# Causal mask by VectorE, three PSUM banks exchanged, and unscaled input rows with the norm's root applied to the products, in a two-layer decoder step

## The reference, cut to what matters

```python
z = rmsnorm(x, g1) @ w_in                     # rmsnorm: x * rsqrt(mean(x*x) + EPS) * g1
u, va = gelu(z[:, :512]), rmsnorm(gelu(z[:, 512:1024]), av_g)
q, k, v = rmsnorm(z_q), rmsnorm(z_k), z_v     # q and k normed per head half of 64
s_a = chunk_mix(va)                           # per 128 rows, a lower-triangular 128 x 128 matrix per head
p = softmax(where(kpos <= qpos, q @ k.T * 0.125, -1e30))   # two score maps per head (m = 0, 1)
o_b = (p0 - lam * p1) @ v
x = x + concat(u * s_a, rmsnorm(o_b)) @ w_out
x = x + hierarchical_moe(rmsnorm(x, g2))      # 16 experts, top 2, rows gathered and scattered through HBM
```

## Time and profile before

| what | value |
|---|---|
| median of 3 runs | 1022.73 us (1018.94 to 1022.89) |
| profiled execution | 1022.66 us |
| its span, first to last instruction | 1020.8 us |
| PE busy | 962.5 us (94%) |
| PE weight loads | 495.4 us (49%) |
| DVE busy | 440.4 us (43%) |
| ACT busy | 233.3 us (23%) |
| POOL busy | 191.5 us (19%) |

### The profile page before, as it was taken

The page is one execution under the profiler, slowest core; times in us unless marked ns, Lnnn a source line. Parts: engine busy times, 40 slices in busy tenths (PEclk is TensorE's granted clock), DMA queues, the critical chain, the costliest instruction groups (busy, mean ns, idle before and its releaser), DMA issues.

```text
span 1020.8 us, 13578 instructions
## 1 busy us (share of the span) xinstructions
PE 962.5 (94%) x4918; PEld 495.4 (49%) x4918; DVE 440.4 (43%) x1154; ACT 233.3 (23%) x483; POOL 191.5 (19%) x265
## 2 busy tenths in 40 slices
PE   6999999999998999999599999999989989999991
PEld 4444455556456444434254344655555554444340
DVE  2403122566346466551343111345563565555523
ACT  2101255542001011111121114555220011111110
POOL 2333201331101111111125031022220011111100
PEclk9999999999998999999899999999999999999996
DMA  8716003342511979998742150134252059799946
GB/s 335 267 31 257 1 1 129 103 146 91 220 42 63 383 259 370 420 421 328 240 144 83 49 209 1 68 109 160 63 208 103 21 222 367 274 381 412 403 153 209
DMA packets 39769, 197.72 MB, mean 194 GB/s; under 512 B 7632, under 2 KB 7760, under 8 KB 23824
## 3 DMA queue, kind: packets, MB, share of 16 engines
q1 hardware_dynamic: 19744, 136.22, 34.0%
q0 software_dynamic: 15888, 45.87, 12.8%
q10 hardware_dynamic: 4064, 14.68, 4.0%
HBM read 177.35 MB, written 29.88 MB: 203 GB/s over the span
## 4 chain that ended last, share of the span: by engine, by line
PE 84%; DVE 6%; DMA 4%; issue 2%; POOL 1%; ACT 1%; POOLq 0%; SPq 0%; ACTq 0%; DVEq 0%
PE ps L673 77%; PE ps L671 6%; DMA cat<-y_rows 1%; DMA x<-in_xp 1%; POOL st L517 1%; PE ps L688 1%; DMA y_rows<-hn,isca 1%; DVE cat L1720 1%; DVE hT L1393 0%; DMA hT<-h_rows,igat 0%; DVE tmp L1542 0%; DVE st L1543 0%; ACT hn L1306 0%; DVE st L1510 0%; DVE o_sb L1530 0%
## 5 line engine op out<-in xcount | busy, mean ns | idle before, releaser
L673 PE MATMUL ps<-ring,hT 128*128 128x512 f32 (+2 forms) x1056 | 382.4, 595 | 2.9 <-DVE hT L1393 2.5
L673 PEld LDWEIGHTS ps<-ring,hT 128*128 128x128 f32 (+2 forms) x1056 | 148.9, 166 | 198.1 <-issue 196.9
L673 PE MATMUL ps<-ring,cat 128*128 128x512 f32 (+2 forms) x560 | 195.4, 596 | 2.6 <-ACT hn L1306 2.4
L673 PEld LDWEIGHTS ps<-ring,cat 128*128 128x128 f32 (+2 forms) x560 | 72.9, 162 | 82.3 <-issue 79.4
L617 POOL DMA_INDIRECT y_rows<-hn,isca x28 | 28.1, 1003 | 250.1 <-ACT hn L1306 219.5
L673 PE MATMUL ps<-hT,ring 128*128 128x512 f32 (+1 forms) x256 | 71.8, 437 | 0.3 <-ACT cat L1194 0.3
L515 POOL TENSOR_SCALAR st<-st 128x1 f32<-128x1 f32 (+3 forms) x60 | 16.3, 272 | 282.2 <-ACT sqj L1150 106.4
L517 POOL TENSOR_TENSOR st<-st,half 128x1 f32<-128x1 f32 (+3 forms) x60 | 62.5, 1042 | 11.6 <-POOL st L515 11.1
L1861 DVE TENSOR_TENSOR hT<-ps,par 128x512 f32<-128x512 f32 x56 | 36.0, 685 | 56.0 <-PE ps L671 55.6
L1414 DVE TENSOR_REDUCE st<-sqj 128x8 f32<-128x512 f32 x20 | 13.5, 681 | 108.3 <-ACT sqj L1165 108.2
L1306 ACT COPY hn<-ps 128x1024 f32<-128x1024 f32 x28 | 28.4, 1013 | 118.3 <-PE ps L673 118.3
(11 more groups left out here) (249 smaller groups left out, 1172.7 us busy)
## 6 DMA issues: line engine op xcount, KB each, us to landing
ring<-in_w SPq DMA_DIRECT2D x82, 1024.0 KB
kc<-in_w SPq DMA_DIRECT2D x12, 1024.0 KB
vc<-in_w SPq DMA_DIRECT2D x10, 1024.0 KB
v<-in_w SPq DMA_DIRECT2D x10, 1024.0 KB
kva<-in_w SPq DMA_DIRECT2D x10, 1024.0 KB
kc<-in_ck POOLq DMA_DIRECT2D x32, 256.0 KB, 3.6
vc<-in_cv POOLq DMA_DIRECT2D x32, 256.0 KB, 3.2
h_rows<-qk ACTq DMA_DIRECT2D x10, 512.0 KB, 2.6
```

The costliest lines, as they stand in the source:

```text
L673: ins = pe.matmul(out, lhsT, rhs, start=start, stop=stop, skip_group_check=loose)
```

## The change

- **Input rows.** PE turns `x` itself, with no `scaled` before it. The root multiplies the products instead: by ACT on the way out of the bank for k, v, q and va (a scale per row), and for the transposed gates u by DVE, which multiplies bank F by a row of roots into `tmp`; ACT's gelu then reads `tmp`. The row of roots on all partitions (`roots`) is made after the keys: DVE scales the identity by each tile's roots (`diagonals`), PE multiplies ones by them into T0 and T1, DVE copies them.
- **Layer change.** PE's identity products wait for the last scatter, and are nine; DVE adds a tile and turns the one before it.
- **Causal mask.** The four mask products are gone; DVE adds the mask in PSUM before the maximum.
- **Banks.** `OT[0]` and `OT[1]`, `OT[2]` are exchanged (T1, T1, T0 for T0, T0, T0), and mix(3) uses T1 for F. ACT's turned probabilities come first in the steps that have a `pT`.
- Tile 1 is loaded ahead of the second weight piece; the output tile 3 is turned one product later; ACT takes the gelus of u0 and u1 after its key and query copies.

```diff
-        OT = {t: spare_turn(4 * t + 9) if t < TP - 1 else f"T{t % 2}" for t in range(NT)}
+        OT = {0: "T1", 1: "T1", 2: "T0", TP - 1: "T1", TP: "T0"}
+        MIX_IN = {t: "F" for t in range(NT)}
+        MIX_IN[TP - 1] = spare_turn([n for n, works in SMALL.items() if ("mix", TP - 1) in works][0])
...
+                    if i == 1 and l == 0:
+                        x_load(1)
...
             def turn_half(stage, t, hf):
-                rows = x[:, t, :] if stage == "x" else hn[:, t % 2, :]
+                rows = x[:, t, :]
...
                 if l:
-                    pe.wait_ge(x_ready.sem, l * NT + 1)
-                    keep_busy(10)
+                    Count.layer = l - 1
+                    pe.wait_ge(*y_out[(NSLOT - 1) % 2].at("y", "m", NSLOT - 1))
+                    Count.layer = l
+                    keep_busy(9)
+
+                def turn_input(t):
+                    if l == 0:
+                        pe.wait_ge(*dve_s.at("blank"))
+                        pe.wait_ge(x_in[t].sem, 16)
+                    turn_rows("h1", t, (x_ready.sem, l * NT + (t + 1)))
...
                 rows("k", 0)
+                pe.wait_ge(*dve_s.at("diagonals"))
+                for t in range(NT):
+                    u, n = ("T0", P) if t < TP else ("T1", NROW)
+                    if t in (0, TP):
+                        claim(u)
+                    mm(bank(u)[:, t % TP * P:t % TP * P + n], ones, diagonals[:, t * P:t * P + n], inc=full[u].inc("roots") if t >= TP - 1 else None)
                 rows("v", 1)
...
-                        mm(bank(u, m)[:, 0:(i + 1) * P], qT[m * DK:(m + 1) * DK, h, here], kT[m * DK:(m + 1) * DK, h, 0:(i + 1) * P])
-                    for stay, move in ((B_ID, B_CAUSAL), (B_SWAP, B_SWAP_CAUSAL)):
-                        for m in range(2):
-                            r = slice(m * DK, (m + 1) * DK)
-                            mm(bank(u, m)[:, here], c16[r, stay], c16[r, move], start=False, loose=True,
-                               inc=full[u].inc("s", n) if (m == 1 and stay == B_SWAP) else None)
+                        mm(bank(u, m)[:, 0:(i + 1) * P], qT[m * DK:(m + 1) * DK, h, here], kT[m * DK:(m + 1) * DK, h, 0:(i + 1) * P],
+                           inc=full[u].inc("s", n) if m else None)
...
-                    if (n, k) == (1, 1):
+                    if (n, k) == (1, 2):
                         turn_out(TP - 1)
...
-                        nc.scalar.copy(dst[:, t, :], bank(u)).then_inc(*read[u].inc("z", name, t))
+                        nc.scalar.mul(dst[:, t, :], bank(u), stat["rs"][:, t:t + 1]).then_inc(*read[u].inc("z", name, t))
...
+                    if n in PT_STEPS:
+                        probs_turned(n - 2)
...
+                vec.memset(ones, 1.0)
+                for t in range(NT):
+                    dve.wait_ge(*pool_c.at("rs1", t))
+                    ins = vec.tensor_scalar(diagonals[:, t * P:(t + 1) * P], ident, stat["rs"][:, t:t + 1], None, ALU.mult)
+                ins.then_inc(*dve_s.inc("diagonals"))
...
+                def scale_gates(name, j):
+                    dve.wait_ge(*full["F"].at(name, j))
+                    if name == "us":
+                        out, src = (a.rearrange("p (m t) -> p m t", m=4)[:, :, 0:NROW] for a in (tmp[:, 0:4 * NROW], bank("F")))
+                        by = across(roots[:, TP * P:TP * P + NROW], 4, NROW)
+                    else:
+                        out, src, by = tmp[:, :], bank("F"), roots[:, 0:TP * P]
...
+                    vec.tensor_tensor(out, src, by, ALU.mult).then_inc(*read["F"].inc(name, j))
...
                     b0 = FIRST[f"S{n % 2}"]
+                    diagonal = ps[:, b0:b0 + 2, i * P:(i + 1) * P]
+                    link(vec.tensor_tensor(diagonal, diagonal, across(c16[:, B_CAUSAL], 2, P), ALU.add))
                     link(vec.tensor_reduce(stat["mx"][:, c:c + 2], ps[:, b0:b0 + 2, 0:(i + 1) * P], AX.X, ALU.max))
...
-                for t in range(NT + 4):
-                    if 2 <= t < NT + 2:
-                        add_high(t - 2)
+                for t in range(NT + 1):
+                    if t < NT:
+                        add_high(t)
```

More of the change, by code:

```diff
@@ L262, in program @@
                   v[:, 0:TP, :].rearrange("p t n -> p (t n)"), kva[:, 0:TP, :].rearrange("p t n -> p (t n)")]
+        diagonals = hn[:, 0, 0:NT * P]
+        roots, ones = hn[:, 1, 0:TOK], hn[:, 1, TOK:TOK + P]
         rows_of = sb("rows_of", [P, NT, E, 4], BF16)
@@ L1185, in _ @@
                 square_heads("q", TP, "S0", LOW)
[L1186 to L1187 removed]
+                nc.scalar.mul(qz[LOW, TP, :], bank("S0")[LOW, :], stat["rs"][LOW, TP:TP + 1])
+                nc.scalar.activation(kva[HIGH, TP, :], bank("S0")[HIGH, :], ACT.Gelu_apprx_tanh, scale=stat["rs"][HIGH, TP:TP + 1]).then_inc(*read["S0"].inc("z", "qva"))
                 act.wait_ge(*read["S0"].at("z", "qva"))
@@ L1266, in _ @@
                         probs(n)
-                    if 2 <= n < len(ATT) + 2:
+                    if 2 <= n < len(ATT) + 2 and n not in PT_STEPS:
                         probs_turned(n - 2)
@@ L1434, in _ @@
                 vec.tensor_reduce(stat["lam"][:, 0:2], groups(tmp[:, 0:2 * DK], 2, DK), AX.X, ALU.add).then_inc(*dve_s.inc("lamdot"))
-                link(vec.memset(hn[:, :, :], 0.0))
+                dve.wait_ge(*full["T0"].at("roots"))
+                vec.tensor_copy(roots[:, 0:TP * P], bank("T0")).then_inc(*read["T0"].inc("roots"))
+                dve.wait_ge(*full["T1"].at("roots"))
+                vec.tensor_copy(roots[:, TP * P:TP * P + NROW], bank("T1")[:, 0:NROW]).then_inc(*read["T1"].inc("roots"))
+                link(vec.memset(hn[:, 0, :], 0.0))
                 for t in range(2, NT):
@@ L1487, in mix @@
                 def mix(t):
-                    dve.wait_ge(*full["F"].at("mix", t))
+                    u = MIX_IN[t]
+                    dve.wait_ge(*full[u].at("mix", t))
                     bs = par[:, PAR["bs"]].rearrange("p (c t) -> p c t", c=4)
                     n = NROW if t == TP else P
-                    s, o = (a.rearrange("p (c t) -> p c t", c=4)[:, :, P - n:P] for a in (bank("F"), tmp[:, :]))
+                    s, o = (a.rearrange("p (c t) -> p c t", c=4)[:, :, P - n:P] for a in (bank(u), tmp[:, :]))
                     bs = bs[:, :, 0:n]
@@ L1500, in mix @@
                         dve.wait_ge(*dve_s.at("mix", t - 1))
-                    vec.tensor_tensor(added, part, bs, ALU.add).then_inc(*read["F"].inc("mix", t))
-                    dve.wait_ge(*read["F"].at("mix", t))
+                    vec.tensor_tensor(added, part, bs, ALU.add).then_inc(*read[u].inc("mix", t))
+                    dve.wait_ge(*read[u].at("mix", t))
                     vec.tensor_tensor(catT[:, 0:4, t * P:t * P + n], o, catT[:, 0:4, t * P:t * P + n], ALU.mult).then_inc(*dve_s.inc("mix", t))
@@ L1612, in _ @@
                             add_out(*j)
+                        elif name != "va":
+                            scale_gates(name, j)
+                    if n == 3:
+                        dve.wait_ge(*act_s.at("us", 0))
+                        link(vec.memset(hn[:, 1, :], 0.0))
                     for name, j in SMALL.get(n, []):
@@ L1682, in _ @@
                 turned(0)
+                scaled(0)
                 head_turned(TP - 1)
-                scaled(0)
                 add_out(1, 1)
```

68 lines of the change are left out of this document (35 added, 33 removed).

## The result

| what | before | after |
|---|---|---|
| median | 1021.43 us (6 runs, 1018.94 to 1022.89) | 1028.37 us (6 runs, 1026.21 to 1029.68) |
| ratio to before | | 1.0071, 95% [1.0055, 1.0087] |
| profiled execution, its span | 1022.66, 1020.8 us | 1029.64, 1027.9 us |
| PE busy | 962.5 us | 966.3 us |
| DVE, ACT busy | 440.4, 233.3 us | 455.7, 240.2 us |

What follows compares the result with a forecast made beforehand. The prediction took PE's stream, 84% of the chain that ended last, as the bound. Terms -1.0 +4.0 -4.0 +2.8 +0.4 gave +2.2; with clock losses of 1.5 and 1.0, +4.7: 1027.4, said as 1027 us, range 1013 to 1036.

Steps and rivals of the forecast that it cites:

- forecast case: Whole kernel: slower, with one or two clock losses, own range 1023 to 1031 us; chance 0.45.
- +2.2: Whole kernel: sum in us of the start, roots, layer change and attention terms, before any clock loss.
- Start, -1.0: Kernel start: the second tile's transposes no longer wait for DVE's scaling, 1.0 us gained.
- Roots' products, layer 0, +4.0: After layer 0's keys: PE waits 2.9 us for the diagonals, then 1.1 us of products; cost 4.0 us.
- Layer 1 has the same slip: After layer 1's keys: PE waits 1.7 us for the diagonals, products take 1.1; cost 2.8 us.
- Change of layer, -4.0: Between layers: warm-up waits only for the last scatter, first product at 511.65 instead of 515.68; 4.0 us gained.
- The attention, +0.2 a layer: Attention steps: mask products saved, DVE additions, bank waits and output turn together cost 0.2 us a layer.
- T1 wait: Last attention step: the last head's transposes wait until DVE has read mix(3) from T1; cost 1.7 us a layer.
- later output turn: Attention's end: turning the output one product later fills a PE wait, 0.8 us gained a layer.
- The clock, +2.5: Half clock after layer 0's roots' wait, 1.5 us, and an even chance of 2 at the layer change, taken as 1.0.
- "clearly slower" rival: Last attention step: two waits of 1.9 us also lower the clock in both layers, 1031 to 1037 us; chance 0.15.
- Faster rival: Claims of F and T1: 0.46 us of slack each keeps the mask addition off PE's path, 1011 to 1014; chance 0.15.

Runs made afterwards that it cites:

- e2: The kernel before with one edit: DVE adds the causal mask in place of PE's four mask products per step; 1024.48 us, ratio 1.0039.
- e10: e5 with nine unread identity products ahead of mix(3), in PE's wait there; 1015.43 us, ratio 0.9946.
- e9: The kernel after with seven unread identity products ahead of mix(3) and seven ahead of the last turn_probs, in both layers; 1023.56 us, ratio 1.0030.
- e3: The kernel after with the layer-change warm-up products written into T0 without a claim of bank J; 1027.83 us, ratio 1.0077.
- e5: The kernel after with the edits of e1, e3 and e4 together, and eleven warm-up products instead of nine; 1018.54 us, ratio 0.9985.
- e8: e5 with the mask given back to PE's products in all 16 steps, DVE adding none; 1014.01 us, ratio 0.9942.
- e11: e6 with seven unread identity products ahead of mix(3), in PE's wait there; 1014.14 us, ratio 0.9934.
- e7: e5 with DVE's mask addition made twice in every step; 1022.81 us, ratio 1.0024.
- e6: e5 with the mask given back to PE's products in steps 3, 7, 11 and 15; 1013.74 us, ratio 0.9935.
- e4: The kernel after with the diagonals' wait and the five roots' products moved behind the next four value products, both layers; 1022.43 us, ratio 1.0028.
- e1: The kernel after with mix(3) put back in bank F instead of T1; 1022.6 us, ratio 1.0028.

## Why the prediction was right, and where its steps were off

1027 was forecast and 1028.4 measured, inside the forecast case's own 1023 to 1031. The direction and the main places (the roots' waits, the claims of F, the two waits of the tail) were right. That the number came so near is in part luck. The terms for the layer change and the attention promised 1.9 and 0.3 too much gain. Against that, the roots cost 1.1 less than forecast, the start gave 0.2 more, and 0.8 was saved behind PE's last product, a place that the forecast didn't have. Without the clock this makes +2.3 for +2.2. The clock added 4.7 for 2.5, mostly at other places. Measured against the profiled 1022.66, 1029.64 is 7.0 more, for 4.7 forecast.

- **Start, -1.0.** The second tile's wait is gone, but it belonged to the profiled execution: e2 has the old start, ACT had the second tile's row at 13.99 instead of 15.36, DVE scaled it at 16.47 instead of 17.84, and there was no wait. A gain was booked from one execution's DMA arrival. From start to start it was 1.2: from the first product to the last tile's first one it took 29.3 us for 30.5. Against it stands the first product, 1.03 later. It was at 12.29 and 12.71 in the two kernels with the old start, and between 12.36 and 13.81 in those with the new one. In both kinds it comes late where the clock was granted in full late: 8.80 us and 12.29 in before, 9.03 and 12.36 in e10, 10.07 and 12.71 in e2, 11.24 and 13.32 in after, 12.00 and 13.81 in e9. So this 1.03 goes with the clock of the execution, and no trace shows a start that the edit itself made later.
- **Roots' products, layer 0, +4.0.** Right in kind. The diagonals were ready at 46.72 (46.6 to 46.8 forecast), but two f32 products are four records, 1.72 us, and I had counted 0.86, so the keys ended at 44.4 and the wait was 2.25 instead of 2.9. From 44.4 to 47.95 it is 3.6. Layer 1 has the same slip: from 548.6 to 550.75 it is 2.1, of which 1.2 are the products, for 2.8. The five scalings took 0.93 for my 0.9. The Trainium skill's 58 cycles and half the columns ("VectorE: DVE Perf Modes", the section on the TRN2 errata) would give, as an estimate, 0.65 for the five, so the trace stands against it.
- **Change of layer, -4.0.** The step that failed. I read ACT's load issues at 503.50 in the earlier trace rows as the moment the warm-up could start, and priced "the scatter has landed" without asking what else `keep_busy` waits for. The claim of J made it -2.1; the missing 1.9 is what e3's first product gains (11.55 us from scatter to product, 13.41 in after). With the claim gone and warm-up products that reach up to the transposes, e5 gets -4.5.
- **The attention, +0.2 a layer.** From the roots' products up to mix(2) the changed kernel gained 0.3 a layer, where I had 0.7 (the list without the T1 wait and without the later output turn, which stand behind mix(2)). The mask products were worth 0.11 to 0.12 a step instead of 0.21, and I had booked seven of them as gain: 0.6 to 0.7 too much. The places were right: waits at F in steps 4, 8 and 12, and the old wait in step 9 to 10 gone. The later output turn was worth 0.86 a layer, for 0.8. The T1 wait was right to 0.2: the tail is longer by 1.5 at full clock (e9), for +1.7. ACT's copies with a root take 0.68 instead of 0.58, the squares 0.69 instead of 0.60; I had called them the same form. The Trainium skill has it ("ScalarE: Activation LUTs", What ACT_TABLE_LOAD costs): each per-partition operand adds about 93 ns. The rows agree, with 0.09 to 0.10 us. No wait of PE in the projections came with it, so nothing hung on it.
- **The clock, +2.5.** Both the size and the places were off. Neither the roots' wait (2.25 us in the midst of dense products) nor the layer change in after cost clock. The tails did, 1.6 and 3.1 (19.79 and 21.36 against e9's 18.2), which was the mechanism of the "clearly slower" rival. That rival had 1031 to 1037, because I added its price on top of a clock loss that didn't come. The late full clock at the start cost 1.0. And 1.4 came back in layer 0's experts stage: half clock at 317 in the earlier trace rows lasted from 316.0 to 322.8, in after from 321.9 to 325.3. e8, e9 and e11 have none there and take 246.8 to 246.9 us for the stage, after 247.5; before took 249.7, of which 0.86 is the output turn. Layer 1's experts lost 0.4 in the same way. Part of what a profile shows as gain or loss is thus which execution it is.
- **Faster rival.** It needed slack of 0.46 per claim. There was none: without the addition (e8) the waits for F are 2.4 us a layer shorter, and a second one (e7) lengthens them by 3.6 of the 3.7 us that it takes at the eight claims.

The verdict on the change by its parts: input rows, layer change and later output turn, well placed and with the mask left to PE (e8), are worth 6 us by the medians; how much of that is the clock of other stages isn't separated. DVE's mask addition in all steps costs 0.5 us per layer in waits at the tail and next to nothing in the body, and two or three times that through the clock; with the wait filled (e10) it is as fast as PE's mask within the error. e6, the mix of both, beats the kernel before by 0.65%.

## What to carry to other kernels

Before booking the gain of an earlier start, list every wait in front of the moved instruction, the bank claims too, and who releases them behind what else. On a PE-bound kernel a wait of about two microseconds can have a second price behind it, the clock; filling it with products that nobody reads is a cheap experiment and can be a cheap remedy (-4 us in e9 and in e10, nothing in e11, where the wait was 1.7). The worth of removed small products is read from start to start between their neighbours with and without them, not from their own starts.

## What was not expected of the hardware

- The same two waits of 1.7 us, 2 us apart, left the clock in full in one layer and brought it to half in the other of one execution (e4). In the traces of the kernels whose tail has a single wait of 1.7 (before, e6, e8) it fell in one of six tails; with one unfilled wait of 2.3 to 2.8, or two of 1.7, in 12 of 14; with the waits filled (e9, e10, e11) in none of six. That activity and not place decides is also what the Trainium skill says ("TensorE: Matmul & The Clock Gate", What's actually happening), and these counts agree; e4 shows that they don't settle the single case. They come from one execution of each kernel.
- The roots' wait, 2.1 to 2.3 us in the midst of dense 128x512 products, left the clock in full in all four traces that have it (after, e1, e3, e9). So the length of a wait alone doesn't decide.
- In e3's profile the warm-up started 3.2 us earlier than in after and ended 0.85 us before the real work, and the clock came back some 3.5 us later behind the scatter. This is one execution of a kernel whose runs lie 8 us apart.
- Four bf16 products of 64 rows behind f32 scores take 0.28 us in their records and cost 0.11 to 0.12, in every step.
